# Delta rule's background work: the query units of head pairs 2 and 3 move from the start of one pair's stretch to the end of the stretch before

## The reference

```python
def hybrid_mixer(h, w_in, ...):
    dn_qkv, dn_z, dn_b, dn_a, sb_q, sb_k, sb_v, gate_a, gate_b = split_cols(h @ w_in)
    qkv = silu(causal_depthwise_conv(dn_qkv, conv_w))      # 4 taps along the tokens
    q, k, v = split(qkv, 3)                                # 8 heads of 128
    o_a = gated_delta_rule_chunked(l2norm(q), l2norm(k), v, g, beta)   # chunks of 64 tokens
    y_a = (rmsnorm(o_a) * silu(dn_z)) @ w_branch_a
    y_b = stick_breaking_attention(rmsnorm(sb_q), rmsnorm(sb_k), sb_v) @ w_branch_b
    return (sigmoid(gate_a) * y_a + sigmoid(gate_b) * y_b) @ w_out
```

## Time and profile before

| | |
|---|---|
| median of the runs | 2415.54 us |
| span of the profiled execution | 2418.1 us (the profile gives no time beside this span) |
| TensorE busy | 2341.3 us, 97% |
| VectorE, ScalarE busy | 1125.0 us (47%), 1113.8 us (46%) |
| GpSimd busy | 1706.9 us (71%) |
| mean granted TensorE clock | 0.995 |
| delta stretches, pairs 0 to 2 | 260.65 to 465.60 us (layer 0), 1084.50 to 1287.90 us (layer 1) |

### The profile page before, as it was taken

One profiled execution on the slowest core, in us unless ns is written; L12 is line 12 of the kernel. 1 busy time (PEld: TensorE's weight loads), 2 busy tenths in 40 slices (PEclk: granted clock), 3 DMA queues, 4 the chain that ended last, 5 costly groups with the idle time before them and its releaser, 6 DMA issues.

```text
span 2418.1 us, 40330 instructions
## 1 busy us (share of the span) xinstructions
PE 2341.3 (97%) x15689; PEld 2132.2 (88%) x15689; DVE 1125.0 (47%) x1947; ACT 1113.8 (46%) x1273; POOL 1706.9 (71%) x1340
## 2 busy tenths in 40 slices
PE   8999899999999999999999999999999999999998
PEld 7888889999988888898899999889898888898887
DVE  3334755432333333365664142333524666433776
ACT  4335444447443443454444654335555335555433
POOL 6998545546799899974455568997545997645996
PEclk9999999999999999999999999999999999999999
DMA  7555323224455555552233344655333555423553
GB/s 240 191 191 164 116 88 105 89 88 141 158 191 190 191 175 191 191 157 88 88 99 102 100 150 162 200 187 172 123 101 115 191 191 169 137 88 124 189 191 131
DMA packets 312357, 359.97 MB, mean 149 GB/s; under 512 B 18660, under 2 KB 291104, under 8 KB 312096
## 3 DMA queue, kind: packets, MB, share of 16 engines
q1 hardware_dynamic: 311866, 357.75, 45.6%
q10 hardware_dynamic: 358, 0.33, 0.0%
HBM read 357.01 MB, written 1.05 MB: 148 GB/s over the span
## 4 chain that ended last, share of the span: by engine, by line
PE 85%; DVE 10%; ACT 2%; issue 1%; POOL 1%; DMA 0%; SPq 0%; DVEq 0%; ACTq 0%
PE ps L751 21%; PE ps L551 21%; PE ps L583 16%; PE ps L588 9%; PE ps L630 3%; PE ps L837 1%; PE ps L790 1%; PE ps L646 1%; PE ps L844 1%; POOL sb_lo L524 1%; DVE sb_kT L1864 1%; PE ps L1125 1%; DVE sb_vT L1864 1%; PE ps L846 1%; PE ps L617 1%
## 5 line engine op out<-in xcount | busy, mean ns | idle before, releaser
L524 POOL TENSOR_TENSOR sb_lo<-sb_raw,sb_hi 128x512 fp32r<-128x512 f32 (+1 forms) x1336 | 1706.7, 1313 | 693.3 <-ACT sb_hi L1226 692.9
L1226 ACT ACTIVATE sb_hi<-sb_raw 128x2048 fp32r<-128x2048 f32 (+3 forms) x341 | 639.1, 1876 | 658.5 <-PE ps L588 349.2
L583 PE MATMUL ps<-sb_hT,sb_hi 128*128 128x512 f32 x1792 | 426.1, 390 | 0.0
L583 PEld LDWEIGHTS ps<-sb_hT,sb_hi 128*128 128x128 f32 x1792 | 332.9, 188 | 66.5
L751 PE MATMUL ps<-sb_hT,sb_hi 128*128 128x256 f32 x2304 | 312.4, 288 | 5.0 <-DVE sb_hT L1993 2.8
L751 PEld LDWEIGHTS ps<-sb_hT,sb_hi 128*128 128x128 f32 x2304 | 286.6, 192 | 11.0 <-DVE sb_hT L1993 3.2
L588 PEld LDWEIGHTS ps<-sb_hT,sb_lo 128*128 128x128 f32 x1792 | 229.8, 191 | 8.7
L1784 DVE TENSOR_TENSOR sb_yinv<-ps,sb_row 128x512 f32<-128x512 f32 x112 | 77.5, 692 | 335.3 <-PE ps L588 335.2
L588 PE MATMUL ps<-sb_hT,sb_lo 128*128 128x256 f32 x1792 | 232.5, 283 | 0.0
L551 PE MATMUL ps<-sb_hi,sb_o_h 128*128 128x512 f32 x560 | 219.8, 393 | 0.9 <-DVE sb_o_l L1791 0.9
L551 PE MATMUL ps<-sb_hi,sb_o_l 128*128 128x512 f32 x560 | 218.8, 391 | 0.0
(11 more groups left out here) (379 smaller groups left out, 3665.2 us busy)
## 6 DMA issues: line engine op xcount, KB each, us to landing
sb_raw<-in_ffn_w_in SPq DMA_DIRECT2D x88, 1024.0 KB, 5.1
sb_raw<-in_w_in SPq DMA_DIRECT2D x78, 1024.0 KB, 5.2
sb_raw<-in_ffn_w_out SPq DMA_DIRECT2D x44, 1024.0 KB, 4.9
sb_raw<-in_ffn_w_up SPq DMA_DIRECT2D x44, 1024.0 KB, 5.1
sb_raw<-in_ffn_w_down SPq DMA_DIRECT2D x22, 1024.0 KB, 4.9
sb_raw<-in_w_out SPq DMA_DIRECT2D x16, 1024.0 KB, 5.1
sb_raw<-in_w_branch_a SPq DMA_DIRECT2D x8, 1024.0 KB, 5.1
sb_raw<-in_w_branch_b SPq DMA_DIRECT2D x8, 1024.0 KB, 5.1
```

Of the source, the lines that this page charges most:

```text
L524: ins = nc.gpsimd.tensor_tensor(lo[:, slot, c], raw[:, slot, c], hi[:, slot, c].bitcast(F32), ALU.subtract)
L583: mm(ps[:, bank + i, :].rearrange("p (h n) -> p h n", h=2), wh[:, c, i * P:(i + 1) * P], hT_both[:, :, c, :], start=c == 0, stop=False, sk ...
L1226: fn(hi[:, slot, 0:width], raw[:, slot, 0:width], ACT.Copy).then_inc(hi_ready, 1)
```

## The change

Two units change place between the entries of `DELTA_BG`. `("q", 2)`, which was the first unit of pair 1's stretch, becomes the last of pair 0's; `("q", 3)`, which was the first of pair 2's, becomes the last of pair 1's. The entries have 6, 6, 6 and 7 units in place of 5, 6, 7 and 7.

```diff
-DELTA_BG = [pair_units(1)[1:] + [("sv", 2), ("sv", 3)], pair_units(2) + [("sq", 0), ("sk", 0)],
-            pair_units(3) + [("sq", 1), ("sk", 1), ("ga", 0)],
+DELTA_BG = [pair_units(1)[1:] + [("sv", 2), ("sv", 3), ("q", 2)],
+            pair_units(2)[1:] + [("sq", 0), ("sk", 0), ("q", 3)],
+            pair_units(3)[1:] + [("sq", 1), ("sk", 1), ("ga", 0)],
             [("sq", 2), ("sk", 2), ("ga", 1), ("ga", 2), ("gb", 0), ("gb", 1), ("gb", 2)]]
```

## The result

The changed kernel takes 2422.74 us (median of 10 runs, 2420.41 to 2426.26) against 2416.16 for the kernel before (10 runs, 2414.45 to 2418.68). The ratio is 1.0026, with a 95% interval of 1.0017 to 1.0034: slower by 6.6 us, a small loss, but the interval leaves out 1. The forecast was +9.7 us, 2425.2, with the range 2418.5 to 2430.

What follows compares the result with a forecast made beforehand. TensorE, busy 97% of the span, bounds the kernel; only its waits in two delta stretches and its clock can move the time. Layers +3.3 and +1.75 give +5.05, clock +4.65: +9.7, 2425.2 us, range 2418.5 to 2430.

Steps and rivals of the forecast that it cites:

- the sum without half clock: Both layers' delta stretches: layer 1 +3.3 us and layer 0 +1.75, together +5.05.
- The bank wait: Step 2 of pairs 1 and 2: v waits for q's second block to leave bank 0, 2.25 us a pair.
- Block one: q's first block on VectorE, between L1912 and L1918: 0.5 + 1.5 us, hidden in a gap of 3.7.
- Pair 0: 20 parts become 24: +3.2 us, from 64.10 to 67.3, with a wait of 1.44 uncovered ahead of L827.
- Pairs 1 and 2 without half clock: 24 parts each: 67.89 + 2.25 - 0.38 = 69.76 us, say 69.7, for each pair.
- levels 0 to 2 look as before: Pairs 1 and 2: k 2's evacuations fall into steps 2 and 3, where q 2's were, so these levels keep their look.
- The wait ahead of uw: Pairs 1 and 2: v 2's evacuations leave steps 10 and 11, so this wait of 0.38 us goes.
- Pair 3: Same plan and unit order as before, predecessor ends with ga, which ScalarE takes out: no change.
- The clock: Half clock behind three of the four new waits, at 1.55 us each: +4.65; bounds none and 6.2.
- Stall, but full clock: Rival: the four waits of 2.25 come but the clock holds: +5.05 us, 2420.6; chance 0.17.
- No bank wait: Rival: q's second block is out before TensorE finishes L827: -3.95 us, 2411.6; chance 0.08.
- Slow L1924: Rival: GpSimd runs beside L1924 in all four, waits of 3.2 and half clock each: +15 us, 2430.6; chance 0.13.

Runs made afterwards that it cites:

- experiment 2: Changed kernel with 16 idle TensorE transposes behind L828 in pairs 1 and 2: 2414.04 us against 2417.36 for the kernel before (0.9991).
- experiment 1: Changed kernel with q 2 and q 3 last but one of their entries, sv 3 and sk 0 last: 2409.86 us against 2417.36 before (0.997).
- experiment 3: Changed kernel with z 2 and z 3 moved one pair sooner in place of q 2 and q 3: 2412.22 us against 2417.36 before (0.9978).
- experiment 5: Kernel before with only q 3 moved, entries of 5, 7, 6 and 7 units: 2421.59 us against 2416.71 (1.0023).
- experiment 4: Changed kernel, but VectorE takes out both blocks of q 2 and q 3 in step 0 of pairs 1 and 2: 2416.32 us against 2417.36 before (0.9996).

## Why the prediction was right, and where it was not

The mechanism was right in place, releaser and size of the new wait. That the time came out in the range is in part luck: the sum without half clock was 7.9 us too high, the half clock 3.2 too low, and the two errors offset each other in part. The time alone doesn't decide it either: 2422.7 lies 2.5 us below the forecast and 2.1 above the rival with full clock; the rows do.

- **The bank wait.** Forecast 2.25 us at the first part of step 2 in four pairs, released by the evacuation of `q`; measured 2.01 to 2.02 of idle time in all four, at L752, released by L1865, and 2.28 by what it delays p0 (experiment 2 against 1). L1925 took 0.69 as forecast, because GpSimd's instructions ended before it (in pair 1 at 338.14, L1925 began at 338.72). Block one was hidden, as said: L828 came 11.2 us after the pair's start in pairs 1 and 2, as it does in experiment 1, where no block stands there.
- **Pair 0.** Forecast 67.3, measured 66.6. The wait that a third part in step 1 had covered is 0.84, not 1.44.
- **Pairs 1 and 2 without half clock.** Forecast 69.76, taken as 69.7; measured 68.45 in experiment 2. This is the step that failed: "levels 0 to 2 look as before". They don't: VectorE's L1933 fell at a better moment, the wait of 0.62 at p1 went, and 0.87 us was paid back. Two terms were mis-sized besides. The wait ahead of uw was put at its idle time, 0.38, but was worth 0.63, as experiment 3 against 1 shows; and L828 comes 11.2 us after the pair's start, not 11.4. These account for the whole: 67.89 + 2.28 - 0.87 - 0.63 - 0.20 = 68.47.
- **Pair 3** was said not to change. It is 0.75 shorter in each layer, and the wait of 0.58 ahead of its L827 is gone. GpSimd was at work from the start of the pair and now begins 5 us into it; VectorE's L1916 and L1921 took 1.51 and 1.86, and now, as L1917 and L1922, 0.69 and 1.10. The rows below are from layer 0, first the kernel before, then the changed one. Experiment 5, where pair 0 is as before and pair 2 has 24 parts, has the same times here and no wait, so it goes with the shorter entry of pair 2; which of its steps does it, no run isolates.

```profile
466.07 10.91 POOL L524 TENSOR_TENSOR sb_lo<-sb_raw,sb_hi 128x512 fp32r<-128x512 f32 x8 [11.37 <-ACT sb_hi L1226]
...
473.97 1.86 DVE L1921 TENSOR_TENSOR sb_levels<-sb_levels,sb_const 128x512 f32<-128x512 f32 x1
```

```profile
473.31 5.49 POOL L525 TENSOR_TENSOR sb_lo<-sb_raw,sb_hi 128x512 fp32r<-128x512 f32 x4 [5.61 <-ACT sb_hi L1227]
...
476.54 1.10 DVE L1922 TENSOR_TENSOR sb_levels<-sb_levels,sb_const 128x512 f32<-128x512 f32 x1
```

- The base without half clock was thus 2 x 0.7 + 4 x 1.25 + 2 x 0.75 = 7.9 us too high: forecast +5.05, while experiment 2 lies 3.3 below the kernel before by the medians (5.05 - 7.9 would be 2.9 below).
- **The clock.** Forecast 4.65, from three of four places at 1.55. All four had half clock in the profiled execution, which is the slowest of the ten, and it cost 7.9: the price from pair 0 was one spell, and pair 1 had a spell twice as long. So the half clock isn't an addition to the loss, it decides the sign: without it the change would be a small gain.
- **Rivals.** "Stall, but full clock" has the price 2420.6 on record; experiment 2 shows that state at 2414. "No bank wait" was forecast at 2411.6, -3.95 us; experiment 1 is that kernel, at -7.5. Both were too slow, by 8.3 and 3.5 us: in both pair 0, pair 3 and the waits ahead of L828 and uw were put too long, and in the first the return at p1 was missing as well. "Slow L1924" didn't occur here, but does in experiment 5.

The gain of the even spread, from experiment 1, adds up: pairs 0 to 2 took 204.95 + 203.40 before and 200.69 + 200.69 after it, 7.0 less, of which 1.55 is the half clock of pair 0, and pair 3 gives 1.5. That is 8.5 by the profiles, 7.5 by the medians. The change takes this gain of 8.5, pays 4 x 1.42 = 5.7 for the bank wait and 7.9 for the half clock: a loss of 5.1, as the two delta stretches show.

What stays open: why the spell of half clock is 6.83 us long in pair 1 and 3.4 in pair 2, in both layers; and how often each place has it. The rows show only that TensorE stood idle longer after the clock had fallen where the spell was long: 1.27 and 0.68 us in pair 1 of the two layers, 0.50 and 0.18 in pair 2. No run varies this by itself. The ten runs of the changed kernel spread over 5.8 us, with mean clocks from 0.995 (2420.41, 2420.89, 2421.20 us) down to 0.992 and 0.993 (2425.14 and 2426.26), so the number or length of the spells differs from run to run.

## What to carry to other kernels

When work is moved that another engine must clear away, ask which engine clears it, at which place of its own order, and who needs the room next; a unit that keeps its bank and its number can still block it at a worse time. On a chain-bound stretch, even out the filling work, but end each stretch with a piece that is taken out of its bank at once, here by ScalarE. And price a new wait of the matmul engine together with the clock behind it: here the wait cost 1.4 us and the half clock 1.3 to 2.7.

## What was not expected of the hardware

- Sixteen useless transposes in a wait of 2.0 us made the kernel faster: the granted clock stayed full in all four places, and pairs of 69.7 to 71.2 us became 68.45.
- Whether half clock follows doesn't depend on the length of a wait alone. The wait of 2.27 in pair 0 was followed by it in one of two layers, in the kernel before and again in experiment 5; a single wait of 1.96 in three of four pairs (experiment 4); two waits, 1.2 and 2.0, in four of four. By the Trainium skill (TensorE: Matmul & The Clock Gate, section HAM oscillation — how this bites in real kernels) a spell costs half its length. As an estimate that gives 3.4 us for the spell of 6.83 in pair 1 of layer 0, where 2.45 was measured, and 1.7 for pair 2, where 1.28 was measured; TensorE worked in only 5.56 and 2.92 us of the two, and half of that, 2.8 and 1.5, is nearer.
- A row's idle time understates what the wait costs: 2.01 us of it at the bank delayed the chain by 2.28, and the 0.38 ahead of uw made the pair 0.63 longer.
- The same VectorE instruction, L1924 or L1925, took 0.69 or 1.64 us, and a stall of TensorE's grew by the difference: 2.01 to 2.96.
